# Gathering the second expert table as 2 picks of 64 tokens instead of 4 picks of 32, with spread weights of 128x64

## What is computed

```python
act = jnp.einsum('bthkd,btd->bthk', u[eb], xb).astype(jnp.float32)
w = (gb * jax.nn.gelu(act, approximate=False)).astype(v.dtype)
return jnp.einsum('bthk,bthkd->btd', w, v[eb])
```

## Time and profile before

| | us |
|---|---|
| median of 3 runs | 3667.61 |
| lowest and highest | 3663.51, 3670.87 |
| span of the profiled execution | 3485.3 |
| the profiled execution's own time | not given apart from the runs |
| TensorE busy (matmuls) | 2938.0 (84%) |
| VectorE busy | 2308.4 (66%) |
| ScalarE busy | 1089.0 (31%) |
| GpSimd busy | 1826.1 (52%) |
| moved | 1089.84 MB, mean 313 GB/s |

### The profile page before, as it was taken

The page is one execution under the profiler, slowest core; times in us unless marked ns, Lnnn a source line. Parts: engine busy times, 40 slices in busy tenths (PEclk is TensorE's granted clock), DMA queues, the critical chain, the costliest instruction groups (busy, mean ns, idle before and its releaser), DMA issues.

```text
span 3485.3 us, 40700 instructions
## 1 busy us (share of the span) xinstructions
PE 2938.0 (84%) x14108; PEld 1972.0 (57%) x14108; DVE 2308.4 (66%) x4988; ACT 1089.0 (31%) x2862; POOL 1826.1 (52%) x1672
## 2 busy tenths in 40 slices
PE   8999998999998677666767536699999889999994
PEld 6878875666656234323423304477776656777771
DVE  3350027888317779989888888966666697666665
ACT  3320024554113333344334222223222232332222
POOL 3242201221003777767776677766556676655566
PEclk9999998999999788888887756799999867999997
DMA  3322235322355999999999999999999999999998
GB/s 143 129 88 94 94 108 190 106 93 97 138 216 205 386 409 400 406 389 394 396 404 387 409 403 383 403 403 409 409 409 410 406 408 394 409 409 409 409 409 347
DMA packets 312861, 1089.84 MB, mean 313 GB/s; under 512 B 33232, under 2 KB 56400, under 8 KB 309600
## 3 DMA queue, kind: packets, MB, share of 16 engines
q0 software_dynamic: 221184, 805.40, 58.6%
q1 hardware_dynamic: 91488, 282.04, 21.3%
HBM read 1051.07 MB, written 36.24 MB: 312 GB/s over the span
## 4 chain that ended last, share of the span: by engine, by line
DMA 22%; PE 19%; DVE 11%; POOL 11%; issue 6%; ACT 1%; POOLq 0%; DVEq 0%; ACTq 0%
DMA arena<-in_u_dram,idx 13%; DMA arena<-in_v_dram,idx_v 9%; PE small L1842 6%; POOL arena L1689 5%; POOL arena L1672 5%; PE acc L1724 4%; PE wide L1859 4%; DVE arena L2258 4%; PE small L1830 1%; DVE idx_v L2491 1%; PE wide L1749 1%; DVE gates_v L2491 1%; DVE arena L2533 1%; PE small L1932 0%; DVE arena L2489 0%
## 5 line engine op out<-in xcount | busy, mean ns | idle before, releaser
L1672 POOL DMA_INDIRECT arena<-in_u_dram,idx x768 | 785.8, 1023 | 618.1 <-DVE act_u L2258 255.5
L1689 POOL DMA_INDIRECT arena<-in_v_dram,idx_v x752 | 796.2, 1059 | 370.8 <-issue 209.7
L1724 PE MATMUL acc<-arena 128*32 128x512 f32 x3008 | 493.1, 786 | 405.7 <-DMA arena<-in_v_dram,idx_v 378.0
L2258 DVE CUSTOM_DVE_ANT_0 arena<-arena,wide 128x1024 f32<-128x1024 f32 x470 | 568.0, 1216 | 132.3 <-DMA arena<-in_u_dram,idx 128.6
L2258 DVE CUSTOM_DVE_ANT_0 arena<-arena,h 128x1024 f32<-128x1024 f32 x298 | 362.8, 1224 | 261.1 <-DMA arena<-in_u_dram,idx 260.4
L1724 PEld LDWEIGHTS acc<-arena 128*32 128x32 f32 x3008 | 101.9, 128 | 661.9 <-issue 571.9
L1842 PE MATMUL small<-pwq 128*128 128x256 f32 x2048 | 471.4, 384 | 1.7 <-ACT memory_tables L2119 1.6
L1842 PEld LDWEIGHTS small<-pwq 128*128 128x128 f32 x2048 | 389.8, 192 | 85.2 <-issue 28.7
L2129 ACT ACTIVATE arena<-small 128x256 f32<-128x256 f32 x128 | 49.3, 385 | 654.2 <-PE small L1842 654.2
L422 PE MATMUL group<-w_nat_high,x_parts 128*128 128x512 f32 x768 | 244.4, 400 | 3.8 <-ACT arena L561 3.8
L2018 ACT ACTIVATE arena<-comb,w_v 128x32 f32<-128x32 f32 x768 | 199.7, 311 | 141.9 <-PE acc L1724 93.9
(11 more groups left out here) (361 smaller groups left out, 4706.4 us busy)
## 6 DMA issues: line engine op xcount, KB each, us to landing
pwq<-in_uT_dram SPq DMA_DIRECT2D x128, 512.0 KB, 9.0
pwq<-in_v_dram SPq DMA_DIRECT2D x128, 512.0 KB, 6.8
arena<-in_w_nat_dram SPq DMA_DIRECT2D x6, 2048.0 KB, 8.4
nat_dram<-stage SPq DMA_DIRECT2D x48, 256.0 KB, 2.2
arena<-in_u_dram,idx POOLq DMA_INDIRECT x768
arena<-in_v_dram,idx_v POOLq DMA_INDIRECT x752, 9.1
scanT_dram<-stage SPq DMA_DIRECT2D x22, 512.0 KB, 2.8
arena<-in_w_tr_dram SPq DMA_DIRECT2D x18, 512.0 KB, 3.8
```

The costliest lines, as they stand in the source:

```text
L1672: pool.indirect_dma_start(out=u_ring[:, g % U_RING, :], out_offset=None, in_=peer_u, in_offset=bass.IndirectOffsetOnAxis(ap=idx[:, t % KEP ...
L1689: pool.indirect_dma_start(out=v_row(g), out_offset=None, in_=peer_v, in_offset=bass.IndirectOffsetOnAxis(ap=idx_v[:, t % KEPT, n:n + 1], a ...
L1724: last = pe.matmul(acc[c * QUAD:(c + 1) * QUAD, half * 512:(half + 1) * 512], spread_row(at), v_row(at)[:, half * 512:(half + 1) * 512], s ...
L2258: dve.tensor_tensor_reduce(out=row, in0=row, in1=against, scale=1.0, scalar=0.0, op0=ALU.mult, op1=ALU.add, accum_out=act_u[:, (n // TOPK) ...
```

## The change

The group of `v` becomes 2 picks of 64 tokens. The weights have 64 columns, a combine comes once in two slots and issues four matmuls into two strips of 64 rows. The spread weights move from the arena to a ring of 16 of their own. The constant `FOUR` keeps what stayed at four (the semaphores of the last 16 gathers). The memory for GpSimd's transfer descriptors is set to 4096. The diff, cut:

```diff
-QUAD = 32
-SIDE = 4
+ROWS = 64
+SIDE = 2
+SPREADS = 16
+FOUR = 4
...
-        u_ring, work, h1, spread_w, vals = carved(shared["arena"], (U_RING * D, 4 * D, D, V_RING * QUAD, 2 * PHEADS * TOPK))
+        u_ring, work, h1, vals = carved(shared["arena"], (U_RING * D, 4 * D, D, 2 * PHEADS * TOPK))
...
-        spread_w = spread_w.rearrange("p (s n) -> p s n", s=V_RING)
+        spread_w = sb("spread_w", [P, SPREADS, ROWS], F32)
...
-        comb = sb("comb", [P, QUAD], F32)
+        comb = sb("comb", [P, ROWS], F32)
...
-            return final_spread[:, final_place(g), :] if final_place(g) >= 0 else spread_w[:, g % V_RING, :]
+            return spread_w[:, g % SPREADS, :]
...
-                        pe.wait_ge(final_landed[final_place(g) // SIDE], 16 * SIDE)
+                        pe.wait_ge(final_landed[final_place(g) // FOUR], 16 * FOUR)
...
-                            last = pe.matmul(acc[c * QUAD:(c + 1) * QUAD, half * 512:(half + 1) * 512],
+                            last = pe.matmul(acc[c * ROWS:(c + 1) * ROWS, half * 512:(half + 1) * 512],
...
-                                gelu_v[r * QUAD:(r + 1) * QUAD, h % 2, :].rearrange("p (b c) -> p b c", c=SIDE)[:, :, c],
-                                act_u[c * QUAD:(c + 1) * QUAD, h % 2, :].rearrange("p (b r) -> p b r", r=SIDE)[:, :, r],
+                                gelu_v[r * ROWS:(r + 1) * ROWS, h % 2, :].rearrange("p (b c) -> p b c", c=SIDE)[:, :, c],
+                                act_u[c * ROWS:(c + 1) * ROWS, h % 2, :].rearrange("p (b r) -> p b r", r=SIDE)[:, :, r],
...
-                    if V_RING <= g < SLOTS - FINAL:
-                        act.wait_ge(v_used, (g - V_RING) // SIDE + 1)
+                    if g >= SPREADS:
+                        act.wait_ge(v_used, (g - SPREADS) // SIDE + 1)
...
-    nc = _bacc.Bacc("TRN2", target_bir_lowering=False, num_devices=1)
+    nc = _bacc.Bacc("TRN2", target_bir_lowering=False, num_devices=1, dynamic_dma_scratch_size=4096)
```

More of the change, by code:

```diff
@@ L1429, in attend_and_retrieve @@
         final_rows = tables[:, :, :, :].rearrange("p a k n -> p (a k) n")
-        final_spread = work[:, 2 * D:2 * D + FINAL * QUAD].rearrange("p (s n) -> p s n", s=FINAL)
         picksT = h1[:, 0:3 * DT].rearrange("p (w t) -> p w t", w=3)
         HALF_D = D // 2
-        emptied = [x[:, 0:SIDE, :].rearrange("p k n -> p (k n)") for x in (idx_v, gates_v, idx)]
+        emptied = [x[:, 0:FOUR, :].rearrange("p k n -> p (k n)") for x in (idx_v, gates_v, idx)]
         emptied = [emptied[0].bitcast(F32), emptied[1], emptied[2].bitcast(F32), work[:, 2 * D + HALF_D:3 * D]]
@@ L1450, in attend_and_retrieve @@
         v_landed = [sem(f"v_landed{i}") for i in range(V_RING)]
-        final_landed = [sem(f"final_landed{i}") for i in range(FINAL // SIDE)]
+        final_landed = [sem(f"final_landed{i}") for i in range(FINAL // FOUR)]
         dot_done = sem("dot_done")
@@ L1687, in gather_v @@
                         pool.wait_ge(v_used, (g - V_RING) // SIDE + 1)
-                    landed = final_landed[final_place(g) // SIDE] if final_place(g) >= 0 else v_landed[g % V_RING]
+                    landed = final_landed[final_place(g) // FOUR] if final_place(g) >= 0 else v_landed[g % V_RING]
                     pool.indirect_dma_start(out=v_row(g), out_offset=None, in_=peer_v,
@@ L2082, in keep @@
                             last = act.activation(
-                                to[r * QUAD:(r + 1) * QUAD, :].rearrange("p (b c) -> p b c", c=SIDE)[:, :, c],
-                                source[c * QUAD:(c + 1) * QUAD, :].rearrange("p (b r) -> p b r", r=SIDE)[:, :, r],
+                                to[r * ROWS:(r + 1) * ROWS, :].rearrange("p (b c) -> p b c", c=SIDE)[:, :, c],
+                                source[c * ROWS:(c + 1) * ROWS, :].rearrange("p (b r) -> p b r", r=SIDE)[:, :, r],
                                 ACT.Copy)
@@ L2354, in regroup @@
                             last = dve.tensor_copy(
-                                to[r * QUAD:(r + 1) * QUAD, :].rearrange("p (b c) -> p b c", c=SIDE)[:, :, c],
-                                source[c * QUAD:(c + 1) * QUAD, :].rearrange("p (b r) -> p b r", r=SIDE)[:, :, r])
+                                to[r * ROWS:(r + 1) * ROWS, :].rearrange("p (b c) -> p b c", c=SIDE)[:, :, c],
+                                source[c * ROWS:(c + 1) * ROWS, :].rearrange("p (b r) -> p b r", r=SIDE)[:, :, r])
                     return last
@@ L2567, in _ @@
                 for c in range(SIDE):
-                    rows = slice(c * QUAD, (c + 1) * QUAD)
+                    rows = slice(c * ROWS, (c + 1) * ROWS)
                     dve.tensor_copy(comb[rows, :], ident[rows, rows]).then_inc(comb_ready, 1)
```

## The result

The changed kernel takes 3814.8 us (median of 4 runs, 3804.8 to 3818.7), the kernel before in the same comparison 3665.6 us: a ratio of 1.0404, 95% interval 1.0374 to 1.0434. It is slower by about 149 us; the forecast was 3748 us, +80. The measured time lies outside the forecast's own range (3720 to 3775) and 0.2 us inside the wide one (3705 to 3815).

A forecast was written before the change was run, and what follows sets the result against it. Transfers bound the gathered stages, with TensorE some 3% behind in the dense runs. Terms: +98 dense runs, -20 buffers, +2 end, about +80 us on 3667.6, so 3748 us; own range 3720 to 3775, wide range 3705 to 3815.

The forecast's parts named there:

- the four cases: Whole time, 3705 to 3815 us: forecast (0.60), clock not rising (0.14), release gain (0.10), strips overlapping in part (0.06).
- The pair's price: TensorE's combine of 2 picks costs 2.05 us, as one of 4 did; bounds 1.1 and 3.7 us.
- Partial overlap: Strips of 64 overlap 1.6 of 2, a pair takes 2.4 us: 45 us more, 3793 us; chance 0.06.
- no overlap: Strips of 64 run one after another, a pair takes 3.7 us: beyond 4100 us; chance 0.02.
- The dense runs: Both dense runs: 131 us of added combine work on TensorE, less 33.1 us idle now, gives +98 us.
- The give-back of the buffers: Stages behind the dense runs: rows gathered ahead into the ring of 8 save time, -20 us for two runs.
- Zero for fronts and choosing: Fronts and choosing stages: transfers hide TensorE's added work in the fronts, a higher clock pays in choosing; 0 us.
- the step in the sum: Whole time: the 182.3 us between profiled span and timed median lie outside the span and stay unchanged.
- 161 of 142: Second choosing: TensorE's work with doubled combines against stage length, in us; a rising clock was expected to cover it.
- The finer release: Gather-only stages: rows freed in twos lift transfers from 398 to 408 GB/s, -25 us, 3723 us; chance 0.10.
- The clock: Choosing stages: TensorE's granted clock rises enough to pay for the pairs, 0 us; otherwise 3781 us, chance 0.14.
- ScalarE, descriptor memory, spread's ring: Each 0 us: spreads growing 0 to 74 ns are hidden, smaller descriptor memory is harmless, removed waits gain nothing.

The follow-up runs named there:

- quads twice: The kernel before with the eight matmuls of each quad issued twice, in the old slots with the old release: 3723.1 us, ratio 1.0200.
- both by four: The changed kernel with two pairs issued together once in four slots and rows of the second table released in fours: 3755.7 us, ratio 1.0254.
- the trace taken again: The kernel before, unchanged, profiled a second time: 3660.6 us, ratio 1.0022, span 3650.0 us.
- half quads: The kernel before with each quad issued as two halves of two strips, once in two slots, rows still released in fours: 3763.9 us, ratio 1.0335.
- the release in twos: The kernel before with quads issued as two halves, once in two slots, and rows also released two at a time: 3823.0 us, ratio 1.0435.
- release by four: The changed kernel with rows of the second table released in fours, pairs still in every second slot: 3772.5 us, ratio 1.0312.
- the ring of 16: The kernel before with spread weights in their own ring of 16 and the smaller descriptor memory: 3643.4 us, ratio 0.9990.

## Why the prediction was right and wrong

**The number: inside its range by luck.** 3814.8 us lies in the range of 3705 to 3815, but none of the four cases that the range was to take in came true. The prediction also named a sign of being wrong, "if the added time lies in the fronts or choosing stages", and half of it does: 55 + 25 + 5 = 85 of 163 us of span.

**The pair's price: right.** 2.05 us with its switches was the forecast, against bounds of 1.1 and 3.7. The traces show 1.94 us, 3.68 at the half clock, and a period of 8.27 us where 8.2 stood. Partial overlap and no overlap are out. The Trainium skill (TensorE: Matmul & The Clock Gate, "Measured speedup vs the span model") would have made it some 2.4 us, an estimate from its 2.38 times for three column strips. The trace does not agree: two strips of 64 run side by side as fully as four of 32 (8 x 0.4375 = 3.5 us of records in 1.87 us from one start to the next, 7.0 in 1.86).

**The dense runs: right.** They hold 61 quads, not 64, since the earlier trace rows begins the second one 26 us before its first block. The pairs cost 236.3 - 121.6 = 114.7 us more, not 131; of it (475 - 457.6) + (482 - 464.7) = 34.7 us (33.1 forecast) were idle. That leaves 80; 45 + 41 = 86 were measured, where each was to grow by "some 35 to 50 us". The rate is 375 GB/s, in the forecast's 375 to 380. By the runs this splits: 57 us are the load (quads twice), the rest the cadence. A pair between two blocks costs 1.94 us, two in a row 1.82 each (both by four: 220.2 us for 966 records of 8 to a pair), and `dense_u` is busy for 472.8 us where it is 465.8 with the quads twice.

**The give-back of the buffers: not seen.** Instead of -20 us the second choosing and the end have +5 and +3. With the load alone (quads twice) they have -5 and +11.

**Zero for fronts and choosing: wrong, and here the 80 us went.** The step that failed is the one for the other stages, "still under the transfers, which hide it", from which I took 0; the changed kernel has +55 and +25 us in the fronts and the first choosing. It rested on the earlier trace rows, where these stages run at 398 and 400 GB/s. In the trace taken again they run at 358 and 348: the transfers are not full there, so full transfers can't be what covers a delay. The root is the step in the sum, "182.3 us above the span, which I take as outside it and unchanged". The gap said that the traced execution was not like the timed ones, and most of it lies in just the stages for which the trace was taken as proof of a cover. For TensorE's load the 0 came true without that cover (quads twice: 1093 and 187 us). What costs time there the prediction had not priced: against the quads twice the half quads add 27 and 7 us by their cadence, and the release in twos another 37 and 21; in the changed kernel the release is 28 and 20.

The reading "161 of 142" for the second choosing was wrong as well, by the same cut in the earlier trace rows. The whole stage in that trace is 175 us, with TensorE busy for 148.2 and combines of 52.1: 200 of 175 at the old clock.

**The finer release: the sign was wrong.** The prediction had it at nothing, with a gain of 25 us as a rival, since "earlier by up to two rows" seemed harmless. It costs 0.9% in the changed kernel and 1.0% in the half quads, each with intervals that don't meet. I said what GpSimd's wait counts, but not what stands behind that wait in its order, the gather of the first table, nor what else the stages wait for: the fronts' matmuls and VectorE's work on them.

**The clock: right.** It rose from 0.66 to 0.76 and from 0.72 to 0.76 in the choosing stages, and to 0.78 and 0.82 with the quads twice, whose choosing stages are no longer than before (187 and 195 us). That fewer pauses are the reason fits the second (TensorE busy for 136.4 of 200 us, then 166.2 of 205), but not plainly the first (139.5 of 188, then 153.8 of 213). **ScalarE, descriptor memory, spread's ring: right**, at +26 ns per spread (bounds 0 and 74), 1.0012 and 0.9990. The end: +1.9 forecast, +3 measured.

The change's 4.0% in sum, step by step through the runs: load 2.0 (quads twice), the pairs' form 0.5 (not told from nothing), cadence 0.6 (both by four to release by four), release in twos 0.9. The two in the middle are each about as large as their uncertainty; the cadence is shown by the half quads against the quads twice, 1.3%, where form and cadence of the pairs have 1.1% together.

**Left open.** How a finer release comes to hold up the fronts' matmuls isn't shown. It is also open why cadence costs anything in the fronts, where TensorE is free for a quarter of the time. No version here beats the kernel before; the ring of 16 equals it.

## What to carry to other kernels

Set the span of the traced execution beside the timed runs first: if they differ by more than a few us, the trace is of another execution, and "the transfers are full here" may hold for it alone. Two strips of 64 columns take TensorE as long as four of 32, so groups of fewer rows in wider strips double its time for the same rows: look where its idle time is less than that, stage by stage. And a buffer that is released sooner is no sure gain where one queue issues for two rings: here the queue's wait moved to the next ring, another chain of the program stood longer, and it cost about 1%.

## What the runs showed of the hardware that was not expected

In every trace but the first, engines pause in the gathered stages for several us, and the trace names no work that they wait for. TensorE's waits put down to `issue`, in the first trace of the kernel before, over the whole span:

```profile
PE mix_bank L981 <- issue: 0.7, 3, 0.4
```

And in the trace taken again, from 1120 us on:

```profile
PE acc L1724 <- issue: 45.4, 17, 7.4
PE small L1830 <- issue: 36.4, 37, 4.4
```

One such place, in the timelines of TensorE and then ScalarE in the trace taken again:

```profile
1669.07 1.09 PE L1731 MATMUL small<-ident,arena 128*128 128x128 f32 x8
1684.96 3.78 PE L1749 MATMUL wide<-memory_tables,arena 128*128 128x512 f32 x4 [14.79 <-issue]
```

```profile
1666.47 0.32 ACT L2018 ACTIVATE arena<-comb,w_v 128x32 f32<-128x32 f32 x1
1683.88 1.02 ACT L2024 ACTIVATE arena<-small 128x1024 f32<-128x1024 f32 x1 [17.09 <-remote]
```

The eight transposes end at 1670.16, and ScalarE's copy of their result begins 13.7 us later. VectorE and GpSimd work on meanwhile. In the traces of the kernel before and of the ring of 16 about half of such pauses recur within a few matmuls of the same place in the program, this one among them; the others don't, and the first trace, of the same program, has none. Their cause was not found, and no run here takes them away. The loading of instructions is not ruled out: its two queues moved the same 1.70 and 0.70 MB in both traces of the kernel before, which says how much was loaded, not when.

Also not expected: a ring with more rows under way made the kernel slower by 1.35%. The smaller descriptor memory had no effect to be seen (1.0012, 0.9990 to 1.0034).
